# Transformer layer on one core: q and k of all four head pairs by block products in nine front rounds, 12 instead of 28 fill pieces, early attention steps in another order

## What is computed

```
h = rms_norm(x, g_pre_mix)
hc, bg, cg, q, k, v = split(h @ w_in, 6)              # each 1024 x 512
y_conv = bg * causal_conv3(cg * hc)
y_attn = band attention, 8 heads of 64, chunks of 64 rows, 8 chunks to the left,
         relative position bias, softmax(scores + bias) @ v
y = concat(group_norm(y_conv), group_norm(y_attn)) @ w_out
x = x + rms_norm(y, g_post_mix)
f = (silu(h2 @ Wg) * (h2 @ Wu)) @ w_ffn_out           # h2 = rms_norm(x, g_pre_ffn)
out = x + rms_norm(f, g_post_ffn)
```

## Time and profile before

| what | value |
|---|---|
| median of 3 runs | 1093.37 us (1093.21 to 1093.54) |
| the profiled execution | 1093.39 us, of it span 1091.6 us |
| TensorE busy | 1082.3 us, 99% |
| VectorE, ScalarE, GpSimd busy | 795.6, 473.5, 150.9 us |
| granted TensorE clock | 0.999 of full speed |

### The profile page before, as it was taken

One profiled execution on the slowest core, in us unless ns is written; L12 is line 12 of the kernel. 1 busy time (PEld: TensorE's weight loads), 2 busy tenths in 40 slices (PEclk: granted clock), 3 DMA queues, 4 the chain that ended last, 5 costly groups with the idle time before them and its releaser, 6 DMA issues.

```text
span 1091.6 us, 15835 instructions
## 1 busy us (share of the span) xinstructions
PE 1082.3 (99%) x5549; PEld 897.8 (82%) x5549; DVE 795.6 (73%) x1247; ACT 473.5 (43%) x802; POOL 150.9 (14%) x255
## 2 busy tenths in 40 slices
PE   8999999999999999999999999999999999999997
PEld 7888888878888888888888888888888888888886
DVE  6878888656767876968777878777787786555584
ACT  6642243356667665643232323323232256444541
POOL 2400000001101122102211211221121110000030
PEclk9999999999999999999999999999999999999999
DMA  7332123470010643517435543743554689777631
GB/s 270 107 126 77 43 58 127 160 251 2 21 59 20 231 158 114 172 50 249 139 118 188 173 154 116 221 140 119 183 175 151 210 322 363 232 232 231 212 115 77
DMA packets 117333, 168.28 MB, mean 154 GB/s; under 512 B 7880, under 2 KB 73432, under 8 KB 117280
## 3 DMA queue, kind: packets, MB, share of 16 engines
q1 hardware_dynamic: 99648, 107.50, 30.5%
q0 software_dynamic: 16464, 55.89, 14.7%
q10 hardware_dynamic: 1168, 4.20, 1.0%
HBM read 121.65 MB, written 49.04 MB: 156 GB/s over the span
## 4 chain that ended last, share of the span: by engine, by line
PE 95%; DVE 3%; DMA 1%; ACT 1%; issue 0%; POOL 0%; SPq 0%; DVEq 0%; POOLq 0%; ACTq 0%
PE psum L1334 35%; PE psum L1361 19%; PE psum L1171 11%; PE psum L934 8%; PE psum L1219 8%; PE psum L1083 4%; PE psum L976 3%; PE psum L948 2%; PE psum L958 2%; PE psum L923 1%; DMA arena<-in_x 1%; PE psum L1067 0%; PE psum L984 0%; PE psum L966 0%; PE psum L1180 0%
## 5 line engine op out<-in xcount | busy, mean ns | idle before, releaser
L1334 PE MATMUL psum<-arena_r,ws 128*128 128x512 f32 x960 | 224.1, 389 | 0.0
L1334 PEld LDWEIGHTS psum<-arena_r,ws 128*128 128x128 f32 x960 | 180.2, 188 | 37.4
L1334 PE MATMUL psum<-hT,ws 128*128 128x512 f32 x720 | 169.9, 389 | 0.0
L1334 PEld LDWEIGHTS psum<-hT,ws 128*128 128x128 f32 x720 | 135.1, 188 | 28.0
L1361 PE MATMUL psum<-hT 128*128 128x512 f32 (+1 forms) x600 | 135.2, 385 | 0.0
L1361 PEld LDWEIGHTS psum<-hT 128*128 128x128 f32 x600 | 111.3, 188 | 22.5
L2536 DVE TENSOR_TENSOR misc<-misc,psum 128x512 f32<-128x512 f32 x100 | 68.5, 685 | 48.3 <-PE psum L1334 46.1
L934 PE MATMUL psum<-hT,ws 128*128 128x512 f32 (+1 forms) x432 | 95.9, 373 | 0.0
L1171 PE MATMUL psum<-arena_r,ws 128*128 128x512 f32 x372 | 86.9, 389 | 0.0
L1814 ACT ACTIVATE ws<-o_raw 128x512 fp32r<-128x512 f32 x40 | 25.1, 628 | 138.5 <-DVE o_raw L2514 138.0
L934 PEld LDWEIGHTS psum<-hT,ws 128*128 128x128 f32 x432 | 72.5, 189 | 13.9 <-issue 2.2
(11 more groups left out here) (272 smaller groups left out, 1566.3 us busy)
## 6 DMA issues: line engine op xcount, KB each, us to landing
raw<-in_w_ffn_in SPq DMA_DIRECT2D x44, 512.0 KB, 4.4
act_scratch<-arena POOLq DMA_DIRECT2D x77, 256.0 KB, 3.2
raw<-in_w_in SPq DMA_DIRECT2D x22, 512.0 KB, 4.1
arena<-in_w_ffn_out POOLq DMA_DIRECT2D x22, 512.0 KB, 5.7
arena<-act_scratch SPq DMA_DIRECT2D x38, 256.0 KB, 3.5
arena<-in_x SPq DMA_DIRECT2D x16, 512.0 KB, 6.2
raw<-in_w_out SPq DMA_DIRECT2D x16, 512.0 KB, 3.4
raw<-act_scratch SPq DMA_DIRECT2D x26, 256.0 KB, 3.3
```

What stands on the lines that cost most here:

```text
L1334: last = mm(blocks(bank), w[:, k * P:(k + 1) * P], b_operand(i, part, k), start=fresh_bank and k == 0 and w is hi and part == 0, stop=k == ...
```

## The change

`FRONT_PAIRS` becomes 4: a ninth front round makes q and k of head pair 3, which also takes a store and a load of them through DRAM. `FILLED` becomes 2, so 16 of the 28 pieces in the attention go; the 12 left stand in steps 4, 6 and 8 and one in step 0 of pair 0. In the early steps the turned exponentials of tile 1 (`turn_p(t, 1)`) move from the end of step 2 to between the scores of tiles 2 and 3; the turned outputs of pair t-2 (`transpose_o`) move to step 1 and to the second halves of the scores' banks, `o_finish` follows them to step 1, as two instructions of 512 columns, ahead of `read_o`; and on ScalarE both exponentials of step 1 now come before the copy of tile 0, and the copy of tile 1 before the exponentials of step 2.

```diff
-    FRONT_PAIRS = 3
+    FRONT_PAIRS = 4
...
-        FILLS = [[1, 1, 1, 1, 1, 0, 1, 0, 1], [1, 1, 1, 1, 1, 0, 1, 0, 1], [1, 1, 1, 1, 1, 0, 1, 0, 1], [1, 2, 1, 1, 1, 0, 1, 0, 0]]
-        TAP_STEPS = (9, 11, 20)
+        FILLS = [[1, 0, 0, 0, 1, 0, 1, 0, 1], [0, 0, 0, 0, 1, 0, 1, 0, 1], [0, 0, 0, 0, 1, 0, 1, 0, 1], [0, 0, 0, 0, 1, 0, 1, 0, 0]]
+        TAP_STEPS = (5, 6, 10)
...
-        OT_BANKS = psum[:, 2560:3584]
+        OT_BANKS = psum[:, 0:2048].rearrange("p (b h c) -> p h b c", h=2, c=512)[:, 1]
...
                     for i in scored(t, s):
+                        if i == 3:
+                            turn_p(t, 1)
+                            if t > 1:
+                                pe.wait_ge(oT_read, t - 1)
                         scores(t, i)
-                        if i == 2 and t > 1:
-                            pe.wait_ge(tile_free, tile(t - 1, NT - 2) + 2)
-                            transpose_o(t - 1, OT_BANKS)
...
-                if s == 0:
+                if s in (0, 2):
                     return
-                if s in (3, 5, 7):
-                    fill(t, s)
+                if s == 1 and t > 1:
+                    pe.wait_ge(biased, unit(t, 4))
+                    transpose_o(t - 1, OT_BANKS)
...
-                if s in (1, 2, 8):
+                if s in (1, 8):
                     fill(t, s)
+                turn_p(t, s - 1)
                 if s == 1 and t > 0:
                     turn_back(t - 1, NT - 2)
-                pe.wait_ge(exp_done, unit(t, 2 * s))
-                if s > 1:
-                    pe.wait_ge(pT_act, tile(t, s - 1))
...
-                transpose_p(t, s - 1)
                 if s in (4, 6):
                     fill(t, s)
+
+            def turn_p(t, i):
+
+                pe.wait_ge(exp_done, unit(t, 2 * i + 2))
+                if i > 0:
+                    pe.wait_ge(pT_act, tile(t, i))
+                if i == 0 and t == 0:
+                    pe.wait_ge(conv_mixed, mixed(LAST - 1))
+                transpose_p(t, i)
...
+                if s == 2:
+                    read_pT(t, 1)
                 if s < NT:
                     exp(t, 2 * s)
-                if s in (3, 5, 7):
+                if s in (1, 2, 3, 5, 7):
                     exp(t, 2 * s + 1)
...
-                if s > 0:
+                if s not in (0, 2):
                     read_pT(t, s - 1)
-                if s < NT and s not in (3, 5, 7):
+                if s in (0, 4, 6):
                     exp(t, 2 * s + 1)
...
-                if s == 0 and t > 0:
+                if s == 1 and t > 0:
                     copy_o(t - 1, NT - 2)
+                    if t > 1:
+                        o_finish(t - 1, OT_BANKS)
+                    read_o(t - 1, NT - 2)
...
-                if s == 2 and t > 1:
-                    o_finish(t - 1, OT_BANKS)
...
-                if s == 1 and t > 0:
-                    read_o(t - 1, NT - 2)
...
+                if len(pair.shape) == 3:
+                    ts(row(t + PAIRS - 1, HALF), pair[:, 0, :], params[:, t - 1, 4:5], None, ALU.mult)
+                    ts(row(t + PAIRS - 1, HALF, HALF), pair[:, 1, :], params[:, t - 1, 4:5], None, ALU.mult).then_inc(oT_read, 1)
```

More of the change, by code:

```diff
@@ L1037, in step @@
                 if s in (3, 5, 7):
+                    fill(t, s)
                     output(t, s - 3)
@@ L1041, in step @@
                     transpose_o(t, PP[1])
-                if s in (1, 2, 8):
+                if s in (1, 8):
                     fill(t, s)
+                turn_p(t, s - 1)
                 if s == 1 and t > 0:
                     turn_back(t - 1, NT - 2)
-                pe.wait_ge(exp_done, unit(t, 2 * s))
-                if s > 1:
-                    pe.wait_ge(pT_act, tile(t, s - 1))
-                if s == 1 and t == 0:
-                    pe.wait_ge(conv_mixed, mixed(LAST - 1))
-                if s == 2 and t > 1:
-                    pe.wait_ge(oT_read, t - 1)
-                transpose_p(t, s - 1)
                 if s in (4, 6):
                     fill(t, s)
+            def turn_p(t, i):
[5 more added lines that the diff above has]
+                transpose_p(t, i)
             def copied(t, i):
@@ L1066, in transpose_o @@
                 for i in range(NT):
-                    last = tr(bank[:, i * P:(i + 1) * P], row(CR, P, i * P), ident[:, :])
+                    to = bank[:, i * P:(i + 1) * P] if len(bank.shape) == 2 else bank[:, i // 4, i % 4 * P:(i % 4 + 1) * P]
+                    last = tr(to, row(CR, P, i * P), ident[:, :])
                 last.then_inc(oT_psum, 1)
@@ L2384, in o_finish @@
                 dve.wait_ge(oT_psum, t)
-                ts(row(t + PAIRS - 1), pair, params[:, t - 1, 4:5], None, ALU.mult).then_inc(oT_read, 1)
+                if len(pair.shape) == 3:
+                    ts(row(t + PAIRS - 1, HALF), pair[:, 0, :], params[:, t - 1, 4:5], None, ALU.mult)
+                    ts(row(t + PAIRS - 1, HALF, HALF), pair[:, 1, :], params[:, t - 1, 4:5], None, ALU.mult).then_inc(oT_read, 1)
+                else:
+                    ts(row(t + PAIRS - 1), pair, params[:, t - 1, 4:5], None, ALU.mult).then_inc(oT_read, 1)
                 dve.wait_ge(oT_read, t)
```

## The result

The changed kernel takes 1100.13 us (median; 1100.06 to 1100.35) against 1093.36 us before: the ratio is 1.0062, with a 95% interval of 1.0045 to 1.008. It is slower by 6.8 us, or 0.6%; forecast was 8.2 us, 1101.6. The profiled execution took 1100.20 us against 1093.39, so it stands for the median.

What follows compares the result with a forecast made beforehand. TensorE's queue was taken as the bound, busy 1082.3 of 1091.6 us. Front, pieces and waits, +19.05 - 23.2 + 2 x 3.2 + 3.6 + 0.6 + 1.7 = +8.2 us, gave 1101.6 us, range 1097.0 to 1105.0.

Steps and rivals of the forecast that it cites:

- The front round: Ninth front round: 84 more matmuls at 0.2267 us add 19.05 us on TensorE; other engines' work and loads add nothing.
- The pieces: Attention: 16 fill pieces leave TensorE's queue at 1.45 us each, -23.2 us.
- Pairs 2 and 3: Steps 1 to 5: a 10.9 us chain from `transpose_o` against 7.7 us of TensorE work, 3.2 us wait a pair.
- 0.4 for the turn behind it: Turn back behind the values of tile 0: a 0.4 us wait, counted only in the case where ScalarE's part binds.
- The tap in pair 2: VectorE, between the biases of tiles 0 and 1: tap 2 (1.27 us) delays `transpose_o`, half covered, +0.6 us.
- Pair 1: No `transpose_o`; chain from the end of pair 0's last values, 11.3 us against 7.7, +3.6 us.
- Pair 0: Early steps: TensorE waits for v's last load and some 0.3 us for bias and exponentials, +1.7 us in all.
- The term for v: Pair 0: v's last load lands at most at 228.7; TensorE, three pieces fewer, arrives at about 227.0 to 227.3.
- hide the chain: Rival, attention: the new order covers the waits, leaving front and pieces, -4.1 us, 1089.3 us; chance 0.08, of which 0.04 faster.
- Only ScalarE's part binds: Rival, early steps: bias of tile 4 does not end last; values of tile 0 wait; +2.3 us, 1095.7; chance 0.10.
- The clock: Rival, early steps of three pairs: granted clock falls to 1.2 of 2.4 GHz, +23, 1125 us; chance 0.02.

Runs made afterwards that it cites:

- the kernel with 28: The changed kernel's new order with three front pairs, 28 pieces and the earlier tap steps again: 1093.79 us against 1093.42 for the kernel before, ratio 1.0003.

## Why the prediction was right

- **The front round:** 19.05 us forecast, 19.00 measured, with no idle in it.
- **The pieces:** 1.45 us each forecast. The attention gave 12.23 us and the waits took 11.1 (next points), so 16 pieces were worth 23.3, 1.46 each. This is what is left over, not a measurement of its own. A stretch without waits bears it out from nearby: from the scores of tile 5 of pair 2 to the first scores of pair 3, where one piece is gone, it was 16.70 us before (302.14 to 318.84) and 15.29 after (312.98 to 328.27), 1.41 less. Without waits the change would have gained 4.3 us; forecast was 4.1.
- **Pairs 2 and 3:** chain 10.9 us forecast, 10.98 measured; wait 3.2 forecast, 3.2 measured. The prediction named three of the four places; the wait for the exponentials of tile 2 stands only in its rival, as "0.4 for the turn behind it". Part of the close fit is luck, since `o_finish` took 0.2 us more than its term and the other links a little less. That the chain ends at the scores of tile 5 without slack is shown by doubling one link, which added its full length three times; that pieces cover it, by the kernel with 28.
- **The tap in pair 2:** 0.6 forecast; 0.77 at L1073 less the joint's 0.17, 0.6.
- **Pair 1:** 3.6 forecast, 3.0 measured. The way from the end of the last values of pair 0 (271.1) to the scores of tile 5 (281.86) took 10.7 us for 11.3, and 7.7 of it is TensorE's own work; the idle times over the joints add up to 2.9. The power took 2.92 us this time; I had carried over the 3.39 of the earlier trace rows, which is one row of one pair and did not come back.
- **Pair 0:** 1.7 forecast, 1.1 measured. The term for v was mis-sized: v landed 1.1 us sooner after the first scores than the longest landing of the earlier trace rows gave, and left 0.4 us of idle where 1.4 was forecast, while the smaller waits for bias, exponentials and `copy_o` made the rest, some 0.7 for 0.3.
- **Sum:** 19.0 - 23.3 + 6.4 + 3.0 + 0.6 + 1.1 = 6.8 us. It closes by construction, as the pieces are what was left over. The forecast was 1.4 us high, 1.2 of it through pairs 1 and 0.
- **The rivals:** the order did not hide the chain. "Only ScalarE's part binds" had its 1.3 and 0.4 us right (1.27 and 0.39), but the turn back and the bias took 1.5 us more a pair. Even on its own condition, a quick power, it fails: with 0.22 us for the power, pair 2 still waited 2.7 us, not 1.7. The clock did not fall in the kernel after; it fell in the one with the power twice and in the old order with 12 pieces. The Trainium skill, "TensorE: Matmul & The Clock Gate", part 1, says that an idle array drops to half its clock, and the trace with the power twice agrees, with 0.50 in the stretch from 287 to 289 us.

## What to carry to other kernels

Work that fills gaps on the busiest engine is not only work: 12 matmuls fewer cost 6.8 us here, because 16 pieces had covered chains that the busy shares did not show. Before such work is taken away, walk the longest chain between two points of that engine's queue, add the links from rows, and compare with the engine's own work on the same way. Shortening one link of such a chain pays only down to what runs beside it: the power lost 2.7 us, and TensorE gained 0.4 a pair.

## What the runs showed of the hardware

- The granted clock can fall inside a busy kernel. With the power twice, TensorE had three waits of 3.7 us; at or right behind each the clock went to 0.50, which cost 1.6 to 2.8 us each on top of the wait.
- It fell at shorter waits too, and not at all of them. In the old order with 12 pieces no wait of pair 3 was over 1.2 us, and the clock fell. Pair 2 of the same kernel had a wait of 1.85 us and a stretch with less work, and the clock stayed at 1.00. That wait in TensorE's loads of pair 2, and the busy time by stretch in pair 2 and then in pair 3:

```profile
304.08 0.47 PEld L948 LDWEIGHTS psum<-ws 64*128 64x128 f32 x6 [1.85 <-DVE nmax L2242]
```

```profile
302.00:304.00 2.00, 0.47 (x4) 0.23 (x3) 1.82 (x8) 0.55 (x3) 0.00 (x0) 1.00 0.00 0
304.00:306.00 2.00, 1.92 (x16) 1.50 (x18) 1.30 (x8) 0.81 (x4) 0.00 (x0) 1.00 0.00 0
...
338.00:340.00 2.00, 0.70 (x6) 0.42 (x4) 1.93 (x2) 1.44 (x4) 0.00 (x0) 1.00 0.00 0
340.00:342.00 2.00, 1.83 (x14) 1.50 (x15) 1.86 (x8) 1.74 (x6) 1.68 (x1) 0.58 0.00 0
342.00:344.00 2.00, 2.00 (x12) 1.67 (x12) 0.88 (x2) 1.42 (x3) 1.22 (x1) 0.56 0.00 0
```

  In pair 3 the way from the values of tile 0 to the scores of tile 5 took 6.89 us (340.17 to 347.06), against 6.26 in pair 2 (308.88 to 315.14). The low clock cost only these 0.6 us, for TensorE then had less to wait for `copy_o` and for the bias of tile 4 (0.36 us of idle, 0.79 in pair 2). The kernel after stayed at 1.00, with 1.4 us as its longest wait. So neither the longest wait nor the emptiest stretch decides alone; what does was not tried.
